# A one-layer hybrid decoder kernel: TensorE's scatter and gather moved from behind the up matmuls to between the gate and the up matmuls of each expert

## The reference, cut to what matters

```python
def run_block(args):
    e, toks, gw = args
    xb = hf[toks]
    gt = jnp.minimum(xb @ w_gate[e] + b_gate[e], SWIGLU_LIMIT)
    up = jnp.clip(xb @ w_up[e] + b_up[e], -SWIGLU_LIMIT, SWIGLU_LIMIT)
    act = (up + 1.0) * gt * jax.nn.sigmoid(SWIGLU_ALPHA * gt)
    yb = act @ w_down[e] + b_down[e]
    return yb.astype(f32) * gw[:, None]
...
out = jnp.zeros((n_tok, dm), f32).at[tok_pad].add(ys.reshape(m_pad, dm))
```

## Time and profile before

| what | value |
|---|---|
| median of three runs | 1368.18 us (1367.65 to 1368.42) |
| span of the profiled execution | 1369.9 us |
| expert loop in it | about 357 to 1327 us |
| TensorE busy | 1198.6 us (87%) |
| VectorE busy | 454.5 us (33%) |
| ScalarE busy | 197.9 us (14%) |
| GpSimd busy | 142.2 us (10%) |
| moved by DMA | 429.86 MB, mean 314 GB/s |

### The profile page before, as it was taken

One profiled execution on the slowest core, in us unless ns is written; L12 is line 12 of the kernel. 1 busy time (PEld: TensorE's weight loads), 2 busy tenths in 40 slices (PEclk: granted clock), 3 DMA queues, 4 the chain that ended last, 5 costly groups with the idle time before them and its releaser, 6 DMA issues. The chain is left out here.

```text
span 1369.9 us, 18957 instructions
## 1 busy us (share of the span) xinstructions
PE 1198.6 (87%) x7686; PEld 503.7 (37%) x7686; DVE 454.5 (33%) x749; ACT 197.9 (14%) x324; POOL 142.2 (10%) x60
## 2 busy tenths in 40 slices
PE   5895552698799999999999999999999999999997
PEld 4574442564333333333333333333333233333333
DVE  6699979826211211211211111111111111112122
ACT  3341210123111010100001000100001001100013
POOL 3187528201000000000000000000000000000000
PEclk9797865799799999999999999999999999999999
DMA  9200310413599999999999999999999999999980
GB/s 333 75 1 0 123 36 0 163 65 130 194 410 410 410 410 410 410 410 410 410 410 410 410 410 410 410 410 410 410 410 410 410 410 410 410 410 410 410 340 31
DMA packets 121194, 429.86 MB, mean 314 GB/s; under 512 B 7920, under 2 KB 18544, under 8 KB 121168
## 3 DMA queue, kind: packets, MB, share of 16 engines
q1 hardware_dynamic: 120848, 428.44, 79.2%
q0 software_dynamic: 320, 1.05, 0.2%
HBM read 428.41 MB, written 1.05 MB: 314 GB/s over the span
## 5 line engine op out<-in xcount | busy, mean ns | idle before, releaser
L1055 PE MATMUL bank<-arena 128*64 128x512 f32 (+5 forms) x5388 | 940.0, 481 | 45.2 <-DMA arena<-in_exp_w_up 37.6
L1055 PEld LDWEIGHTS bank<-arena 128*64 128x64 f32 (+4 forms) x5388 | 310.7, 128 | 650.8 <-issue 495.2
L204 PE MATMUL bank<-arena 64*64 64x64 f32 (+4 forms) x1552 | 160.4, 301 | 52.4 <-DVE arena L701 44.9
L204 PEld LDWEIGHTS bank<-arena 64*64 64x64 f32 (+2 forms) x1552 | 123.3, 176 | 90.0 <-DVE arena L701 46.4
L1295 DVE TENSOR_SCALAR arena<-bank 128x512 f32<-128x512 f32 x32 | 22.1, 691 | 241.6 <-PE bank L1055 241.6
L1305 DVE COPY arena<-bank 128x512 f32<-128x512 f32 x32 | 22.1, 692 | 234.9 <-PE bank L1055 234.9
L1246 ACT ACTIVATE arena<-arena 128x512 f32<-128x512 f32 x32 | 20.1, 630 | 525.6 <-DVE arena L1290 525.6
L1290 DVE TENSOR_SCALAR arena<-bank 128x512 f32<-128x512 f32 x32 | 22.1, 691 | 198.1 <-PE bank L1055 198.1
L1249 ACT ACTIVATE arena<-bank 128x256 f32<-128x256 f32 x32 | 12.3, 384 | 339.9 <-PE bank L1345 339.9
L1266 DVE TENSOR_TENSOR arena<-bank,par 128x512 f32<-128x512 f32 x33 | 22.8, 692 | 89.1 <-PE bank L1055 89.1
L204 PE MATMUL bank<-arena,con 128*128 128x256 f32 (+1 forms) x32 | 17.7, 704 | 30.9 <-ACT arena L412 18.2
(11 more groups left out here) (250 smaller groups left out, 634.3 us busy)
## 6 DMA issues: line engine op xcount, KB each, us to landing
arena<-in_exp_w_gate SPq DMA_DIRECT2D x128, 1024.0 KB, 18.4
arena<-in_exp_w_down SPq DMA_DIRECT2D x128, 1024.0 KB, 18.4
arena<-in_exp_w_up SPq DMA_DIRECT2D x128, 1024.0 KB, 18.4
arena<-in_w_in SPq DMA_DIRECT2D x8, 1024.0 KB, 12.3
arena<-in_w_out SPq DMA_DIRECT2D x4, 1024.0 KB, 7.0
arena<-in_ple_w_gate SPq DMA_DIRECT2D x4, 1024.0 KB, 18.4
arena<-in_xT SPq DMA_DIRECT2D x1, 1024.0 KB, 5.7
arena<-in_lora SPq DMA_DIRECT2D x1, 1024.0 KB, 13.1
```

The lines of the kernel that those rows point to most:

```text
L204: return nc.tensor.matmul(out, lhsT, rhs, start=start, stop=stop, skip_group_check=True)
L1055: return nc.tensor.matmul(out, lhsT, rhs, start=start, stop=stop, skip_group_check=True)
```

## The change

The scatter and the gather, with the waits that stand ahead of them, go from behind the up matmuls to the place between the gate and the up matmuls (`m == 0` is the gate). The transposes stay behind the up matmuls, and the down matmuls now follow them directly. No instruction is added or taken away, no other engine's code changes, and the waits name the same counts as before.

```diff
                         last = mm(bank[hf * 64:hf * 64 + 64, :], pick[0:E, :], bias[0:E, m, hf * HF:(hf + 1) * HF], False, True)
                     last.then_inc(s[done], 1)
 
-                pe.wait_ge(s["gT_ready"], n + 1)
-                pe.wait_ge(s["y_ready"], n + 1)
-                scatter().then_inc(s["scattered"], 1)
+                    if m == 0:
+                        pe.wait_ge(s["gT_ready"], n + 1)
+                        pe.wait_ge(s["y_ready"], n + 1)
+                        scatter().then_inc(s["scattered"], 1)
+                        pe.wait_ge(s["hot_ready"], 2 * n + 4)
+                        gather()
 
                 pe.wait_ge(s["pg_ready"], 2 * n + 2)
                 for t in range(TT):
@@
                     last = nc.tensor.transpose(GATE[:, k * P:(k + 1) * P], up[:, k * P:(k + 1) * P], ident)
                 last.then_inc(s["actT_done"], 1)
 
-                pe.wait_ge(s["hot_ready"], 2 * n + 4)
-                gather()
                 pe.wait_ge(s["actT_ready"], n + 2)
                 pe.wait_ge(s["gT_ready"], n + 2)
```

## The result

| | before | after |
|---|---|---|
| median | 1368.07 us (1367.65 to 1368.42) | 1420.92 us (1419.87 to 1421.50) |
| ratio | | 1.0383, 95% interval 1.0366 to 1.0400 |
| span of the profiled execution | 1369.9 us | 1419.1 us |
| first and last copy of the down result (L1305) | 391.26, 1326.28 | 390.45, 1375.45 |

The kernel became 3.8% slower. The forecast was 1387.6 us with a range up to 1405, so the direction was right and the size was not; 1420.9 is close to the 1420 us of rival (B), falls of the clock at most experts.

What follows compares the result with a forecast made beforehand. Weight transfers pace mid-loop at 30.72 us a turn; after the change TensorE, at 30.60, would end last. Median 1368.2 + 16.0 for longer turns + 3.4 for two clock falls = 1387.6 us, range 1379 to 1405.

Steps and rivals of the forecast that it cites:

- rival (B): Expert loop: the clock falls at most experts, transposes keeping it up less; 36 us of falls, 1420 us; chance 0.12.
- What bounds the kernel: Mid-loop, weight transfers set the pace at 30.72 us a turn; TensorE on its own needs 28.19 us.
- The moved parts and the two bare pauses: Gate to up gains 3.52 us; up to down, bare waits for VectorE and ScalarE leave 3.02; turn 30.60 us.
- My lower bound of 0.05: Between up and down: with 0.05 us for each of TensorE's two wakings, the gap is 2.86 us.
- The lead: Loop: TensorE runs 32 turns against the DMA's 31, so at 30.60 us a turn it ends last, +16.0 us.
- (A): TensorE's pace with bare waits sets the end, none to six or so clock falls: 1384.2 + 0 to 10; chance 0.80.
- The clock: Bare stretch between up and down: two falls of 1.7 us each, 3.4 us, within bounds of 0 and 54.
- the nearest row: At 304 to 307 us: pauses of 0.48 and 1.45 us, then clock 0.51 for 3.4 us, 1.7 us lost.
- (C): Between up and down: gap only 2.50 us, DMA still sets the end, not slower, about 1368 us; chance 0.05.
- (D): Between up and down: gap 3.4 us or more, wakings 0.3 each, 1396 us without falls; chance 0.03.

Runs made afterwards that it cites:

- The kernel with a longer turn and no pause: Kernel before plus 2.15 us (as planned) of useless dense matmuls a turn, between the activation's transposes and the gather: 1384.44 us, ratio 1.0125.
- the filled one: Kernel after plus useless matmuls in both bare pauses, one of 64x512 in the first and one of 256 columns in the second: 1378.89 us, ratio 1.0085.
- the one with the second pause filled: Kernel after plus one useless matmul of 256 columns in the second pause alone, the first pause of 1.15 us left: 1386.49 us, ratio 1.0127.

## Why the prediction was wrong

- **What bounds the kernel: right.** Before, the transfers at 30.72 us a turn with TensorE's own turn at 28.19; after, no wait for a DMA in the loop.
- **The moved parts and the two bare pauses: right in kind, 0.09 us long in each gap.** Between gate and up lie 470.76 - 459.31 - 8.02 = 3.43 us (forecast 3.52), between up and down 481.71 - 470.76 - 8.02 = 2.93 (3.02). The second is short because TensorE wakes 0.06 and 0.05 us after VectorE and ScalarE, where I had taken 0.13 for both, from the one start ahead of the loop; that is 0.15 us less, of which 0.06 come back because the four transposes took 0.66 and not 0.60. My lower bound of 0.05 was nearly right. The start of the first turn takes 0.14 us in the kernel after too (VectorE done at 359.77, matmuls from 359.91), so it is that place that differs, for a reason not looked for, and the earlier trace rows were the better pattern. Why the first gap is 0.09 short was not looked for either.
- **The lead: right.** A turn of 30.42 us, under the transfers' 30.72, still put TensorE last. The kernel with a longer turn and no pause shows this by itself. Since 31 turns multiply each error, 0.18 us a turn made 5.6 us: without falls the kernel takes 1378.9 (the filled one), where (A) without falls said 1384.2. The sum also counted the profiled execution of before as 1.7 us above its median where it was 3.5; that moved nothing, since only differences were taken from it.
- **The clock: the step that failed.** "I take two falls, 3.4 us, near the lower end." There were 19, and they were worth 42.0 us by the turns and 42.0 by the run with the pauses filled. One fall cost 2.2 us on average and not 1.7, since ten of the 19 lasted 6.8 us. In the terms of the sum the falls make +38.6 us (42.0 for 3.4) and the turns -5.6, together 33.0 of the 33.3 us that the forecast was short by. The mechanism and the place had been named, and the nearest row, the fall behind pauses of 0.48 and 1.45 us, was a match in total (1.93 us there, 1.84 here). I set against it the dense work around and one longer pause without a fall, and chose the low end of a term whose ends were 0 and 54 us. Both rows were true: whether a pause is followed by a fall changes from one turn to the next with the very same pauses. One miss and one hit gave no ground for two falls of 32; they were no measure of how often either, so the range was too narrow at the top.
- **Rival (B)** came close to the measured time, but by two errors that cancel: 36 us of falls for 42, and 16 us of turns for 10. That it came close is luck. Its reason, that transposes keep the clock up less, was not borne out.
- **Rivals (C) and (D)** are out: no wait for up chunks, and wakings of 0.05 us.

Open: why the first four turns had no fall, what fixes the cycle of three turns, why the pause of 2.31 us of the earlier trace rows had no fall behind it while 1.15 us in the loop often has, and why the kernel with the scatter alone moved has more falls (21) from one pause of 1.15 us than the one with the second pause filled (7). The work behind the pause differs, a gather there and the down matmuls here, but this was not tried by itself.

## What to carry to other kernels

Where an engine and the transfers have nearly the same time per turn, ask how many turns each has left to do. Data loaded ahead gives the transfers less to do than TensorE, so TensorE's turn can decide although it is a little shorter than theirs. The break-even worked out here is 30.08 us, not 30.72; the runs lie on both sides of it, 29.56 hidden and 30.42 not. When two phases wait for other engines, the odd jobs of TensorE (here scatter and gather) were worth more as cover for these waits than between gate and up, where they covered nothing. And count the idle time that a move uncovers not only by its length: 1.84 us a turn cost 42 us more through the clock, and a single useless matmul of 0.86 us in the longer pause took that away.

## What the runs showed of the hardware

- A pause of 1.15 us in a stream of matmuls that is otherwise dense was followed by the 1.2 GHz level in 7 to 21 of 31 turns; one of 0.69 us alone (the gather moved, two traces) in none of 31. The fall lasted 3.4 or 6.8 us and cost 1.3 to 3.0 us of a turn. A longer pause is not always followed by one, though: behind 2.31 us in the first part of the program the clock was 1.00.
- f32 transposes back to back for 3.1 us in each turn did not lower the clock (1.00 from 380 to 1330 us).
- A matmul with 64 columns of f32 weights by 512 columns took 0.86 us when it had no partner (two in a row 1.93 us, one 1.07), while two of them for the two halves of the output partitions took little more together (18 in 8.02 us, 0.89 a pair).
- The start of the loop varied between the profiled executions, although the kernels don't differ ahead of it. Two executions of the same kernel (the gather alone moved) had their first down mark at 386.57 and 391.90 us and took 1365.84 and 1370.83 us. The times of before in the later comparisons spread as much, 1365 to 1372 us (no trace of those shows the reason), so differences of 0.1% can't be told here from a few runs.
